# RMSNorm statistics laid out by token, and recurrent heads normalised one at a time, in a hybrid encoder block

## What is computed

```
def rmsnorm(x, g):  return x * rsqrt(mean(x*x, axis=-1) + 1e-6) * g
def modulate(h, shift, scale):  return h * (1 + scale) + shift
h = modulate(rmsnorm(x, norm_g[0]), sh1, sc1)
x = x + 0.5 * g1 * swiglu(h, w_ffn1_in, w_ffn1_out)          # d_ff = 2816
h = modulate(rmsnorm(x, norm_g[1]), sh2, sc2)
q, f_fwd, f_bwd, i, g, aq, ak, av = split(h @ w_mix_in)
o_hgrn: bidirectional gated recurrence, 4 heads of 128; then per head
        o = o * rsqrt(mean(o*o, over its 128 features) + 1e-6) * norm_g * silu(g)
o_attn: windowed attention, 8 query heads of 64
x = x + g2 * (concat(o_hgrn, o_attn) @ w_mix_out)
h = modulate(rmsnorm(x, norm_g[2]), sh3, sc3)
x = x + 0.5 * g3 * swiglu(h, w_ffn2_in, w_ffn2_out)
```

## Time and profile before

| | us |
|---|---|
| median of 3 runs | 1144.74 (1144.17 to 1145.28) |
| span of the profiled execution | 1142.6 |
| PE busy | 1097.7 (96%) |
| DVE busy | 535.2 (47%) |
| ACT busy | 417.8 (37%) |
| POOL busy | 2.9 |
| granted TensorE clock, mean | 0.984 |

### The profile page before, as it was taken

The page is one execution under the profiler, slowest core; times in us unless marked ns, Lnnn a source line. Parts: engine busy times, 40 slices in busy tenths (PEclk is TensorE's granted clock), DMA queues, the critical chain, the costliest instruction groups (busy, mean ns, idle before and its releaser), DMA issues.

```text
span 1142.6 us, 12546 instructions
## 1 busy us (share of the span) xinstructions
PE 1097.7 (96%) x5023; PEld 880.3 (77%) x5023; DVE 535.2 (47%) x607; ACT 417.8 (37%) x498; POOL 2.9 (0%) x14
## 2 busy tenths in 40 slices
PE   7699999999999989999998999979999999999998
PEld 4488888888888868778885778758888888888886
DVE  5854545454454565335449984455223223242323
ACT  4542333333232243225246774224333233232221
POOL 0000000000000000000000000000000000000000
PEclk9899999999999989999999999899999999999999
DMA  8755554644354424222310001122332322323212
GB/s 341 291 184 175 193 200 167 220 158 172 133 199 179 129 61 146 97 74 74 111 38 1 2 1 38 39 73 77 107 110 73 110 96 88 110 75 110 87 60 74
DMA packets 89480, 133.46 MB, mean 117 GB/s; under 512 B 10569, under 2 KB 73413, under 8 KB 89318
## 3 DMA queue, kind: packets, MB, share of 16 engines
q1 hardware_dynamic: 89208, 130.82, 33.6%
q10 hardware_dynamic: 238, 2.17, 0.5%
HBM read 128.78 MB, written 4.19 MB: 116 GB/s over the span
## 4 chain that ended last, share of the span: by engine, by line
PE 89%; DVE 6%; ACT 3%; issue 2%; SPq 0%; DMA 0%; POOL 0%; ACTq 0%; DVEq 0%; POOLq 0%
PE bank L1190 27%; PE bank L1192 27%; PE bank L1191 27%; PE bank L1498 1%; PE bank L1228 1%; PE bank L1253 1%; DVE rinv L853 1%; DVE a_diag L1098 1%; DVE qp_both L1081 1%; DVE z L1081 1%; PE bank L1481 1%; PE bank L1216 1%; ACT kc L703 0%; ACT lg L678 0%; PE bank L1359 0%
## 5 line engine op out<-in xcount | busy, mean ns | idle before, releaser
L1190 PE MATMUL bank<-h_hi,w_hi 128*128 128x512 f32 x976 | 385.3, 395 | 19.5 <-DVE h_lo L864 18.1
L1191 PE MATMUL bank<-h_lo,w_hi 128*128 128x512 f32 x976 | 382.9, 392 | 0.0
L1192 PE MATMUL bank<-h_hi,w_lo 128*128 128x512 f32 x976 | 382.9, 392 | 0.0
L788 DVE TENSOR_TENSOR w_lo<-w_raw,w_hi 128x2048 fp32r<-128x2048 f32 x83 | 190.3, 2292 | 338.6 <-ACT w_hi L523 338.6
L523 ACT ACTIVATE w_hi<-w_raw 128x2048 fp32r<-128x2048 f32 x83 | 158.9, 1915 | 467.4 <-PE bank L1192 467.4
L1190 PEld LDWEIGHTS bank<-h_hi,w_hi 128*128 128x128 f32 x976 | 185.6, 190 | 62.3 <-issue 12.6
L1192 PEld LDWEIGHTS bank<-h_hi,w_lo 128*128 128x128 f32 x976 | 185.2, 190 | 39.3
L1191 PEld LDWEIGHTS bank<-h_lo,w_hi 128*128 128x128 f32 x976 | 185.8, 190 | 38.3
L1190 PE MATMUL bank<-a_hi,w_hi 128*128 128x512 f32 x352 | 139.4, 396 | 0.0
L1192 PE MATMUL bank<-a_hi,w_lo 128*128 128x512 f32 x352 | 139.0, 395 | 0.0
L1191 PE MATMUL bank<-a_lo,w_hi 128*128 128x512 f32 x352 | 139.0, 395 | 0.0
(11 more groups left out here) (161 smaller groups left out, 756.8 us busy)
## 6 DMA issues: line engine op xcount, KB each, us to landing
w_raw<-in_w_ffn_in SPq DMA_DIRECT2D x44, 1024.0 KB, 5.2
ada<-in_w_ada SPq DMA_DIRECT2D x30, 1024.0 KB, 4.9
w_raw<-in_w_ffn_out SPq DMA_DIRECT2D x22, 1024.0 KB, 4.8
w_raw<-in_w_mix_in SPq DMA_DIRECT2D x11, 1024.0 KB, 5.0
ada_first<-in_w_ada SPq DMA_DIRECT2D x6, 1024.0 KB, 17.7
x_nat<-in_x SPq DMA_DIRECT2D x1, 2048.0 KB, 15.2
bias_shear<-rowpad ACTq DMA_DIRECT2D x1, 2048.0 KB, 8.8
w_raw<-in_w_mix_in SPq DMA_DIRECT2D x8, 256.0 KB, 4.3
```

What stands on the lines that cost most here:

```text
L788: ve.tensor_tensor(w_lo[n % 2][:], raw[n % 2][:], as_f32(w_hi[n % 2][:]), ALU.subtract).then_inc(wlo_done, 1)
L1190: te.matmul(out_ap, wh, xh, start=first, stop=False)
L1191: te.matmul(out_ap, wh, xl, start=False, stop=False)
L1192: return te.matmul(out_ap, wl, xh, start=False, stop=last)
```

## The change

1. A norm's sums are laid out by token. The weight is a 128x128 block of `sq` (128 features by 128 tokens), the moving operand one column of ones: four matmuls per square, each giving one column of 128 tokens' sums. Root and reciprocal work on 128x4. Four further matmuls (`norm_spread`) with a column of the reciprocals, broadcast, as the weight and the identity moving give the 512 reciprocals on all partitions, in a second bank, `nm.spread`, from which `norm_t` reads. The spread stands behind `ada_sum(1)` in norm 0 and behind the 16 matmuls of `ada_acc2` in norm 1.
2. `load_sqrt`, a root of one column, stands ahead of the squares of each norm and of the heads' roots.
3. The five adds of norms 1 and 2 move from DVE to GpSimd (`norm_adds`).
4. The first stage behind norms 0, 1 and 2 is `stage_k8_first`: per k it waits for h_hi, does four matmuls, waits for h_lo, does the other two.
5. The recurrent heads are summed, rooted, spread and normalised one by one (`o_sum`, `o_root`, `o_spread`, `o_norm`, `o_hi`, `o_lo`), in written-out orders on PE, ACT and DVE; the attention half of output stage 0 is cut into four pieces between them. Output stage m uses banks 4 to 7.

The core of the diff:

```diff
...
+            def norm_adds(nm):
+                for q in range(1, NADD):
+                    pool.wait_ge(nm.sq, q + 1)
+                    if q > 1:
+                        pool.wait_ge(nm.acc, q - 1)
+                    d, before = nm.order[q], nm.order[q - 1]
+                    nc.gpsimd.tensor_tensor(sq[:, d, :], sq[:, d, :], sq[:, before, :], ALU.add).then_inc(nm.acc, 1)
+
+            norm_adds(norms[1])
             pool.wait_ge(stage_done, N_MIXOUT)
             nc.gpsimd.memset(a_diag[:], 0.0).then_inc(a_zero, 1)
+            norm_adds(norms[2])
...
+            def load_sqrt():
+                sc.activation(warm[:], eps_t[:], ACT.Sqrt)
+
             def norm_stats(nm, q0=0):
+                load_sqrt()
                 for q in range(q0, DT):
                     norm_square(nm, q)
                 a.wait_ge(nm.ss, 1)
-                sc.activation(rt[:], nm.bank[:], ACT.Sqrt, bias=eps_t[:], scale=1.0 / D).then_inc(nm.rt, 1)
+                sc.activation(rms[:, nm.r, 0, :], nm.bank[:, 0:TT], ACT.Sqrt, bias=eps_t[:], scale=1.0 / D
+                              ).then_inc(nm.rt, 1)
...
-            o_square(HH - 1)
-            a.wait_ge(oh_ss, 1)
-            sc.activation(rth[:], bank[4][0:HH, :], ACT.Sqrt, bias=eps_t[0:HH, :], scale=1.0 / P).then_inc(oh_rt, 1)
-            for h in range(HH):
+            def o_root(h):
+                a.wait_ge(oh_ss, h + 1)
+                sc.activation(rms_o[:, h, 0, :], bank[h][:, 0:TT], ACT.Sqrt, bias=eps_t[:], scale=1.0 / P
+                              ).then_inc(oh_rt, 1)
+            def o_hi(h):
                 a.wait_ge(oh_m, h + 1)
                 sc.activation(h_hi[:, h, :], z[:, Z_Q + h, :], ACT.Copy).then_inc(mx_hi, 1)
+            load_sqrt()
+            o_root(0)
+            o_square(HH - 2)
+            o_root(1)
+            o_hi(0)
+            o_square(HH - 1)
+            o_root(2)
+            o_hi(1)
+            o_root(3)
+            o_hi(2)
+            o_hi(3)
...
             def norm_root(nm):
                 v.wait_ge(nm.rt, 1)
-                ve.reciprocal(rinv[:], rt[:]).then_inc(nm.rinv, 1)
+                ve.reciprocal(rms[:, nm.r, 1, :], rms[:, nm.r, 0, :]).then_inc(nm.rinv, 1)
 
             def norm_t(nm, d):
                 if d == 0:
-                    v.wait_ge(nm.rinv, 1)
+                    v.wait_ge(nm.bc, 1)
                     v.wait_ge(fac_done[nm.r], 1)
-                ve.scalar_tensor_tensor(tmod[:, d, :], xT[:, d, :], fac[:, nm.r, d:d + 1], rinv[:],
+                ve.scalar_tensor_tensor(tmod[:, d, :], xT[:, d, :], fac[:, nm.r, d:d + 1], nm.spread[:],
                                         ALU.mult, ALU.mult).then_inc(nm.t, 1)
...
-                    if not last and 2 <= q <= NADD:
-                        norm_add(norms[1], q - 1)
...
-            o_scale(HH - 1)
-            v.wait_ge(oh_rt, 1)
-            ve.reciprocal(rrh[:], rth[:]).then_inc(oh_rr, 1)
-            for h in range(HH):
+            def o_root(h):
+                v.wait_ge(oh_rt, h + 1)
+                ve.reciprocal(rms_o[:, h, 1, :], rms_o[:, h, 0, :]).then_inc(oh_rr, 1)
...
+            o_root(0)
+            o_scale(HH - 2)
+            o_root(1)
+            o_norm(0)
+            o_scale(HH - 1)
+            o_norm(1)
+            o_lo(0)
+            o_root(2)
+            o_lo(1)
+            o_norm(2)
+            o_root(3)
+            o_lo(2)
+            o_norm(3)
+            o_lo(3)
...
+            def stage_k8_first(s, banks, nm):
+                for k in range(DT):
+                    pe.wait_ge(nm.hi, k + 1)
+                    cols = [k * 2 * P + cc * P for cc in range(2)]
+                    for cc in range(2):
+                        te.matmul(banks[cc][:], w_hi[s][:, cols[cc]:cols[cc] + P], h_hi[:, k, :],
+                                  start=(k == 0), stop=False)
+                        te.matmul(banks[cc][:], w_lo[s][:, cols[cc]:cols[cc] + P], h_hi[:, k, :],
+                                  start=False, stop=False)
+                    pe.wait_ge(nm.lo, k + 1)
+                    for cc in range(2):
+                        ins = te.matmul(banks[cc][:], w_hi[s][:, cols[cc]:cols[cc] + P], h_lo[:, k, :],
+                                        start=False, stop=(k == DT - 1))
                 ins.then_inc(stage_done, 1)
...
-                ins = te.matmul(nm.bank[:], ones[:], sq[:, nm.order[q], :], start=(q == first), stop=(q == DT - 1))
+                for t in range(TT):
+                    ins = te.matmul(nm.bank[:, t:t + 1], sq[:, nm.order[q], t * P:(t + 1) * P], ones[:, 0:1],
+                                    start=(q == first and t == 0), stop=(q == DT - 1 and t == TT - 1),
+                                    skip_group_check=True)
...
+            def norm_spread(nm):
+                pe.wait_ge(nm.rinv, 1)
+                for t in range(TT):
+                    ins = te.matmul(nm.spread[:, t * P:(t + 1) * P],
+                                    rms[:, nm.r, 1, t:t + 1].to_broadcast([P, P]), ident[:], start=True, stop=True)
+                ins.then_inc(nm.bc, 1)
...
             pe.wait_ge(xT_act, DT)
             ada_sum(1)
+            norm_spread(norms[0])
...
             pe.wait_ge(acc_step, 72)
             for t in range(2 * DT):
-                ins = te.matmul(bank[5][:, t:t + 1], ada_acc2[:, t // DT, t % DT * P:(t % DT + 1) * P], ones[:, 0:1],
+                ins = te.matmul(bank[6][:, t:t + 1], ada_acc2[:, t // DT, t % DT * P:(t % DT + 1) * P], ones[:, 0:1],
                                 start=True, stop=True)
             ins.then_inc(ada_mm, 1)
+            norm_spread(norms[1])
...
+            def o_sum(h):
+                pe.wait_ge(o_sqd, h + 1)
+                pe.wait_ge(o_scl, h + 1)
+                for t in range(TT):
+                    ins = te.matmul(bank[h][:, t:t + 1], o_sq[:, h, t * P:(t + 1) * P], ones[:, 0:1],
+                                    start=True, stop=True)
+                ins.then_inc(oh_ss, 1)
...
             far2(0)
             far2(1)
-            for h in range(HH):
-                values(h)
-                if h + 2 < HH:
-                    far2(h + 2)
...
+            values(0)
+            far2(2)
+            values(1)
+            far2(3)
+            o_sum(0)
+            values(2)
+            o_sum(1)
+            o_spread(0)
+            values(3)
+            o_spread(1)
...
+            o_sum(2)
             pe.wait_ge(wlo_done, N_MIXOUT + 1)
             pe.wait_ge(o_lod, 1)
-            pe.wait_ge(o_scl, HH)
-            out_part(0, range(HH, DT))
-            pe.wait_ge(oh_rr, 1)
-            for h in range(HH):
-                te.matmul(bank[(5, 6, 7, 1)[h]][:], ident[0:HH, h:h + 1].to_broadcast([HH, P]), rrh[:],
-                          start=True, stop=True).then_inc(oh_bc, 1)
+            out_part(0, range(HH, HH + 1))
+            o_sum(3)
+            out_part(0, range(HH + 1, HH + 2))
+            o_spread(2)
+            out_part(0, range(HH + 2, HH + 3))
+            o_spread(3)
+            out_part(0, range(HH + 3, DT))
...
             for q in range(NADD - 1, DT):
                 norm_sum(norms[2], q)
+            norm_spread(norms[2])
...
```

More of the change, by code:

```diff
@@ L164, in build @@
     ind_qk = at("ind_qk", [P, 18], f32, take(72))
-    ind_h = at("ind_h", [P, 7], f32, take(28))
     lb_t = at("lb_t", [P, 8, 8], f32, take(256))
@@ L174, in build @@
     st = at("softmax_stats", [P, 5, 32], f32, take(640))
+    rms = at("rms", [P, 3, 2, TT], f32, take(96))
+    rms_o = at("rms_o", [P, HH, 2, TT], f32, take(128))
+    warm = at("warm", [P, 1], f32, take(4))
     region = take(0)
@@ L267, in __init__ @@
             def __init__(self, r):
-                self.r, self.bank = r, bank[(0, 4, 4)[r]]
+                self.r, self.bank, self.spread = r, bank[(0, 4, 4)[r]], bank[(6, 5, 5)[r]]
                 self.order = FFN_ORDER if r == 1 else tuple(range(DT))
@@ L989, in _ @@
             v.wait_ge(ada_mm, 8)
-            ve.tensor_tensor(modv[:, 7 * DT:9 * DT], bank[5][:, 0:2 * DT], vec[:, 7 * DT:9 * DT], ALU.add
+            ve.tensor_tensor(modv[:, 7 * DT:9 * DT], bank[6][:, 0:2 * DT], vec[:, 7 * DT:9 * DT], ALU.add
                              ).then_inc(ada_out, 1)
@@ L1192, in three, with stage_k8 @@
                 return te.matmul(out_ap, wl, xh, start=False, stop=last)
-            def stage_k8(s, banks, h_ready=None):
-                steps = [(cc, k) for cc in range(2) for k in range(DT)]
-                if h_ready is not None:
-                    steps = [(cc, k) for k in range(DT) for cc in range(2)]
-                for cc, k in steps:
-                    if h_ready is not None and cc == 0:
-                        pe.wait_ge(h_ready, k + 1)
-                    col = k * 2 * P + cc * P
-                    ins = three(banks[cc][:], w_hi[s][:, col:col + P], w_lo[s][:, col:col + P],
-                                h_hi[:, k, :], h_lo[:, k, :], k == 0, k == DT - 1)
```

(51 more changed lines are left out.)

34 lines of the change are left out of this document (10 added, 24 removed).

## The result

The changed kernel takes 1149.0 us (median of 6, 1147.14 to 1149.43), the one before 1144.45 (median of 6, 1143.46 to 1145.28): ratio 1.0037, 95% interval 1.0026 to 1.0049. It is slower by 4.5 us where 3.7 was forecast. The profiled spans are 1147.6 and 1142.6 us, the mean granted clocks 0.974 and 0.984.

What follows compares the result with a forecast made beforehand. TensorE was taken as the bound (89% of the chain), with 18.1 us of waits before three norm-fed stages. Terms +5.1 + 5.7 - 3.7 - 3.4 = +3.7 gave 1148.4 us from 1144.74; range 1138 to 1152.

Steps and rivals of the forecast that it cites:

- One-column sums do not hold the clock: Norms' square sums: the clock falls to 1.2 GHz about 3 us after wide work, a matmul then taking 0.43 us.
- Rival (a): Norms' sums: one-column matmuls count as work and the clock holds; total -9.3 us, so 1135.4; chance 0.22.
- Norm 0, +5.1: Start of the kernel: exposed table load and low-clock sums outweigh the removed long reciprocal; a loss of 5.1 us.
- Norm 1, +5.7: After FFN 1: the GpSimd add chain, then low-clock ada_acc2 matmuls ahead of the spread; a loss of 5.7 us.
- (b): Norm 1: GpSimd adds as fast as VectorE, 0.68 us each; total -0.4, 1144.3 us; chance 0.15 with other partial relief.
- (c): Norm 1: GpSimd adds far slower, 2.2 us each, so every sum runs low; total +9.7, 1154.4 us; chance 0.08.
- Tail, -3.7: Recurrent heads' tail to the end of the first output stage: 26.0 us instead of 29.7, clock holding; a gain of 3.7.
- Norm 2, -3.4: After the output projection: sums, root and reciprocal end earlier, PE starting at 766.1 instead of 769.57; a gain of 3.4 us.
- Attention and recurrence, 0 forecast: Attention and recurrence, whose code is unchanged: no time lost or gained, 0 us.

Runs made afterwards that it cites:

- experiment 2: The changed kernel with the 16 one-column ada_acc2 matmuls ahead of norm 1's sums; 1143.17 us, ratio 0.9994 to the kernel before.
- experiment 1: The changed kernel with the norms' sums moving 128 columns of ones instead of one; 1138.82 us, ratio 0.9949 to the kernel before.
- experiments 2 and 3: Changed kernel with ada_acc2's matmuls ahead of norm 1's sums (1143.17 us); changed kernel with norms 1 and 2's adds back on VectorE (1146.83 us).
- e9_pad64: The kernel before with 64 unused bytes ahead of `region`, no instruction changed; 1144.32 us, ratio 1.0005.
- experiments 1 to 4: Changed kernel with 128-column sums (1138.82 us), ada_acc2 matmuls first (1143.17), adds on VectorE (1146.83), or no early norm 0 table load (1145.32).
- e10_pad128: The kernel before with 128 unused bytes ahead of `region`, no instruction changed; 1138.13 us, ratio 0.9953.
- e8_best: Changed kernel with 128-column sums, late norm 0 table load, norm 1's adds on VectorE, ada_acc2's matmuls in pieces; 1129.49 us, ratio 0.9878 to before.

## Why the prediction came out as it did

The sign and the mechanisms were right. That the total came within 1 us was partly luck: by the table the terms missed by -1.1 (norm 0), +1.5 (norm 1), +1.6 (unchanged code), -0.6 (tail) and -0.1 (norm 2), which sum to +1.3.

**One-column sums do not hold the clock: right**, and it decided the sign. Rival (a) forecast the high clock through them; it is refuted by the clock of 0.53 with PE fully busy, by the fall without a stall in experiment 2, and by experiment 1, where the clock came back under 128 columns.

**Norm 0, +5.1: right in mechanism.** The clock fell at 30.7 (forecast 31.3), the first tmod came at 46.34 (47.7), PE started at 50.00 (51.3), released by w_lo. The fall is 0.6 early and the rest 1.3 to 1.4, most of it because the x transposes ended at 26.76 in this execution and at 27.91 in the earlier trace rows; from their end PE's start is 5.0 later than before. In experiments 2 and 3, where the fall came 5.0 after the end of the transposes and not 4.0, the same count gives 3.8. So the agreement to 0.1 is more than one execution can bear.

**Norm 1, +5.7: right in mechanism, too small by 1.5.** Counted from before's times (less the 4.0 of norm 0), the adds ended at 418.0 instead of 417.4: their durations of 1.29 are as taken (and near 1.33, the estimate made from the ratio of 1.96 in the Trainium skill's "GPSIMD Engine Reference", section 3.1), but one starts 1.41 to 1.45 us after the other, each waiting for the semaphore of the last. The handover is the largest of three terms sized too small, 0.6. The sums took 4.1, not 3.7: they began 0.7 late, the fall came at 419.3 (forecast 419), and so fewer of them ran high. L1381 took 6.8 as forecast, the spread 2.1 for 1.9. First tmod at 431.1 instead of 429.8, PE 6.6 later instead of 5.3; e9_pad64 has the same 11.05 before PE's start as the earlier trace rows, so this 6.6 stands, while what the first stage adds to it varies with the execution (7.2 against before, 5.7 against e9_pad64). Rivals (b) and (c) fall with the 1.29.

**Tail, -3.7: right, 4.3 measured.** No fall of the clock, as forecast. A sum took 0.81 and a spread 0.80 to 0.98, and the bubbles of 0.1 that I had added to each change of width are in these already.

**Norm 2, -3.4: right**, 3.4 by PE's gap.

**Attention and recurrence, 0 forecast, +1.6 in the profiled execution: missed.** There the clock is low once more, in unchanged code:

```profile
638.30:641.70 3.40, 3.40 (x13) 0.50 0.00 0
```

No profile of experiments 1 to 4 shows a fall there; each has one earlier in the recurrence, as before has. That such falls come and go with the same instructions is shown by e9_pad64 (see the result). The six runs of the changed kernel lie in two groups, two at 1147.1 and 1147.4, four at 1148.9 to 1149.4, which would fit a fall that comes in some of them. That is argued, not shown: of the timed runs only the mean clock is known (0.976 and 0.978 in the faster two, 0.974 to 0.976 in the others).

Of the small edits hidden in the diff, the tensors that moved `region` by 256 bytes cost nothing, but I had not asked. At 128, by the 5.9 us between e10_pad128 and its kernel before, they would have turned the loss into a gain of about 1: an estimate, not run.

## What to carry to other kernels

Before turning a vector engine's wait into matrix work, ask what clock that work will run at: full occupation by narrow matmuls was not enough here, and widening the moving operand to 128 columns, with 127 of them wasted, paid 7.9 us in the norms. Cut narrow work into pieces between wide matmuls, as in the tail and in e8_best. Before crediting one stage with a microsecond, look whether a fall of the clock elsewhere came or went: here that was worth 1.5 to 2 us in code that no edit touched. When an edit moves the allocation, compare the pitch of matmuls in stages that it does not touch before crediting the edit.

## What the hardware showed that I had not expected

- The place of a region in SBUF sets the pitch of 128x512 matmuls: 226.7, 228.9 or 233.3 ns, up to 5.9 us of this kernel (ratio 0.9953).
- A float32 matmul record with 128 moving columns costs no more than one with one column at the same clock (64 in 7.41 us in e8_best, 0.116 each; the earlier trace rows have 0.11), and keeps the clock.
- GpSimd adds 128x512 in 1.29 us, 1.9 times VectorE's 0.68, and 1.40 apart in a chain.
